# Half of a tile transpose moved from TensorE to VectorE in two places of a two-block fp32 layer

## The reference, cut to what matters

```python
# block 1
mixed = (jax.nn.sigmoid(gate_a) * (o_nsa @ w_branch_a)
         + jax.nn.sigmoid(gate_b) * (z @ w_branch_b))
x = x + mixed @ w_out
# block 2
h = h + (g_conv * y_conv + g_attn * y_attn) @ w_mix_out
```

## Time and profile before

| what | value |
|---|---|
| median of 3 runs | 908.96 us (908.59 to 909.35) |
| the profiled execution | 908.91 us |
| its span, first to last instruction | 907.1 us |
| PE busy | 899.0 us, 99% |
| PE weight loads busy | 773.6 us, 85% |
| DVE busy | 682.9 us, 75% |
| ACT busy | 550.0 us, 61% |
| POOL busy | 33.3 us, 4% |
| granted TensorE clock, mean | 0.999 |

### The profile page before, as it was taken

How to read it: one execution, slowest core, us unless ns; L and a number is a source line. 1 busy time by engine, 2 the same in 40 slices (tenths; PEclk the granted TensorE clock), 3 DMA queues, 4 the chain that set the end, 5 groups by cost and what they waited for, 6 DMA issues and landing times.

```text
span 907.1 us, 13640 instructions
## 1 busy us (share of the span) xinstructions
PE 899.0 (99%) x5005; PEld 773.6 (85%) x5005; DVE 682.9 (75%) x1289; ACT 550.0 (61%) x954; POOL 33.3 (4%) x41
## 2 busy tenths in 40 slices
PE   9999999999999999999999999999999999999997
PEld 7888877788888888888889998888889988888886
DVE  6878975368776666667899999999976776666666
ACT  7756877745654445446666557786845755744454
POOL 0400000000000000000001010010000000000000
PEclk9999999999999999999999999999999999999999
DMA  9955445565555555556798888577564377555551
GB/s 334 317 158 169 147 143 166 184 229 186 165 185 197 198 187 203 194 196 202 225 247 257 195 244 251 136 216 221 188 222 164 99 209 247 189 186 186 186 186 46
DMA packets 95442, 178.22 MB, mean 196 GB/s; under 512 B 7889, under 2 KB 17937, under 8 KB 95121
## 3 DMA queue, kind: packets, MB, share of 16 engines
q1 hardware_dynamic: 92128, 166.35, 56.1%
q0 software_dynamic: 2880, 10.49, 6.1%
q10 hardware_dynamic: 368, 0.52, 0.2%
HBM read 164.69 MB, written 1.05 MB: 183 GB/s over the span
## 4 chain that ended last, share of the span: by engine, by line
PE 97%; DVE 1%; DMA 0%; ACT 0%; issue 0%; SPq 0%; DVEq 0%; ACTq 0%
PE pb L496 95%; PE pb L500 1%; PE pb L710 1%; DVE wlo L1763 1%; DMA raw<-in_w_first 0%; DVE KP L1967 0%; ACT whi L1151 0%; DVE KD L1944 0%; ACT QKV L1151 0%; SPq L426 0%; ACT P L1151 0%; DVE X L2513 0%; DVE ST L1954 0%; DVE CC L2067 0%; DVE MSQ L2551 0%
## 5 line engine op out<-in xcount | busy, mean ns | idle before, releaser
L1763 DVE TENSOR_TENSOR wlo<-raw,whi 128x1024 fp32r<-128x1024 f32 (+1 forms) x278 | 329.2, 1212 | 105.3 <-ACT whi L1151 104.9
L1151 ACT ACTIVATE whi<-raw 128x1024 fp32r<-128x1024 f32 (+2 forms) x304 | 309.1, 1039 | 133.0 <-PE pb L496 120.4
L496 PE MATMUL pb<-XT,whi 128*128 128x512 f32 (+2 forms) x1264 | 285.2, 354 | 1.0 <-DVE CC L2067 1.0
L496 PE MATMUL pb<-whi,ZO 128*128 128x512 f32 (+1 forms) x776 | 239.6, 388 | 0.0
L496 PEld LDWEIGHTS pb<-XT,whi 128*128 128x128 f32 (+1 forms) x1264 | 204.3, 189 | 24.0 <-ACT whi L1151 1.2
L496 PEld LDWEIGHTS pb<-whi,ZO 128*128 128x128 f32 x776 | 145.3, 188 | 29.3
L496 PE MATMUL pb<-XT,wlo 128*128 128x256 f32 (+1 forms) x1032 | 167.5, 282 | 0.0
L496 PE MATMUL pb<-whi,XT 128*128 128x512 f32 (+1 forms) x544 | 165.8, 390 | 0.2 <-ACT whi L1151 0.2
L496 PEld LDWEIGHTS pb<-XT,wlo 128*128 128x128 f32 (+1 forms) x1032 | 153.0, 190 | 13.1
L496 PE MATMUL pb<-wlo,ZO 128*128 128x512 f32 (+1 forms) x388 | 148.9, 388 | 0.0
L496 PEld LDWEIGHTS pb<-whi,XT 128*128 128x128 f32 x544 | 101.1, 188 | 21.3 <-issue 0.9
(11 more groups left out here) (255 smaller groups left out, 648.1 us busy)
## 6 DMA issues: line engine op xcount, KB each, us to landing
raw<-in_w_in SPq DMA_DIRECT2D x105, 512.0 KB, 4.8
raw<-in_w_ff SPq DMA_DIRECT2D x64, 512.0 KB, 5.8
raw<-in_w_up SPq DMA_DIRECT2D x32, 512.0 KB, 4.6
raw<-in_w_down SPq DMA_DIRECT2D x32, 512.0 KB, 4.8
wlo<-raw POOLq DMA_DIRECT2D x20, 512.0 KB, 6.6
raw<-in_w_branch_b SPq DMA_DIRECT2D x8, 512.0 KB, 5.4
raw<-in_w_out SPq DMA_DIRECT2D x8, 512.0 KB, 4.1
raw<-in_wx_kv SPq DMA_DIRECT2D x8, 512.0 KB, 6.0
```

Of the source, the lines that this page charges most:

```text
L496: return e.matmul(o, l, r, start=start, stop=stop, skip_group_check=True)
L1151: return e.activation(o, i, ACT.Copy, scale=scale)
L1763: e.tensor_tensor(wlo[u % NW][:, 0:c], raw_tile(u)[:, 0:c], whi[u % NW][:, 0:c].bitcast(F32), ALU.subtract).then_inc(lo, 1)
```

## The change

The first half of the mixed rows (j = 0, 1; columns 0 to 511) of both blocks no longer goes through TensorE. VectorE transposes it in 32x32 blocks from `GB` (`GC2`) into a new SBUF tile `HB`, whose space is free at both times. One instruction takes 32 partitions: it reads partition group a (32a to 32a + 31) of all four k-tiles and both token tiles, 256 elements of each partition, and writes partition group b, so 16 instructions (a, b = 0 to 3) do a half. They stand in three parts of 5, 5 and 6 at the first three units of `b1_wb1` (`b2_wc1`), each part ahead of that unit's `make_lo`. `make_t_hi` and `make_t_lo` of j = 0 and 1 read `HB` instead of the banks and both move to the step of the fourth unit, on ScalarE and on VectorE. The second half stays as it was. `TURNED` renumbers the semaphore counts.

```diff
@@ TensorE, turn_block1 (turn_block2 alike)
                 yield
-                for j in range(2):
-                    e.wait_ge(mixed, 2)
-                    turn_tiles(T_M1, j, GB)
                 for _ in range(3):
                     yield
...
@@ ScalarE, make_t_hi
-                e.wait_ge(*((turned, 4 * TURN[s] + j + 1) if s != T_FFN else tile_at[f"xo{j // 2}", 2 * (j % 2) + 1]))
+                by_blocks = s in BLOCKS and j < 2
+                e.wait_ge(*((t_blocks, BLOCKS.index(s) + 1) if by_blocks else (turned, TURNED[s, j]) if s != T_FFN else
+                            tile_at[f"xo{j // 2}", 2 * (j % 2) + 1]))
...
-                    copy(d[:, :, 0, :], PB[4 + j][:, :].rearrange("p (k n) -> p k n", k=2)).then_inc(t_hi, 1)
+                    copy(d[:, :, 0, :], HB[:, 2 * j:2 * j + 2, :] if by_blocks else
+                         PB[4 + j][:, :].rearrange("p (k n) -> p k n", k=2)).then_inc(t_hi, 1)
...
@@ VectorE
+            def half_blocks(src, part):
+                d = HB.rearrange("p k (t n) -> p k t n", t=2)
+                v = src.rearrange("p (t k n) -> p k t n", t=2, k=8)
+                for m in range((0, 5, 10)[part], (5, 10, 16)[part]):
+                    a, b = m // 4 * 32, m % 4 * 32
+                    i = e.transpose(d[b:b + 32, :, :, a:a + 32], v[a:a + 32, 0:4, :, b:b + 32])
+                if part == 2:
+                    i.then_inc(t_blocks, 1)
...
@@ VectorE, turn_block1 (turn_block2 alike, with mixed 6 and GC2)
-                yield
+                e.wait_ge(mixed, 2)
+                half_blocks(GB, 0)
+                yield
+                half_blocks(GB, 1)
+                yield
+                half_blocks(GB, 2)
                 yield
                 for j in range(2):
                     make_t_lo(T_M1, j, XT)
-                    yield
+                yield
                 yield
```

More of the change, by code:

```diff
@@ L42 @@
 END_PARTS = (((1, 1, 0, 512), (1, 2, 512, 1024)), ((0, 1, 0, 320), (1, 3, 640, 1024), (0, 2, 320, 640)))
-TURN = {s: i for i, s in enumerate((T_M1, T_2, T_MIX, T_M2, T_XA, T_FFN))}
+BLOCKS = (T_M1, T_M2, )
+TURNED = {sj: i + 1 for i, sj in enumerate((s, j) for s in (T_M1, T_2, T_MIX, T_M2, T_XA) for j in range(4)
+                                           if s not in BLOCKS or j >= 2)}
 GAIN = {T_X: "norm1", T_MEM: "normmem", T_2: "norm2", T_MIX: "normmix", T_XA: "normx", T_FFN: "normffn"}
@@ L111, in build @@
         XS = work(W0 + 4096, "XS", 2048)
+        HB = work(W0 + 2608, "HB", 1024)[:, :].rearrange("p (k n) -> p k n", k=4)
         XG = work(W0 + 16232, "XG", 2056)
@@ L380, in build @@
         z_hi, z_lo = sem("z_hi_made"), sem("z_lo_made")
-        gate, mixed = sem("gates_made"), sem("mixed")
+        gate, mixed, t_blocks = sem("gates_made"), sem("mixed"), sem("half_turned_by_blocks")
         right, h_sq, h_hi, h_lo = sem("right_half_copied"), sem("h_squared"), sem("h_hi_made"), sem("h_lo_made")
@@ L764, in turn_block2 @@
                 yield
-                for j in range(2):
-                    e.wait_ge(mixed, 6)
-                    turn_tiles(T_M2, j, GC2, (ln_var, 1))
                 for _ in range(3):
@@ L771, in turn_block2 @@
                     e.wait_ge(mixed, 8)
-                    turn_tiles(T_M2, j, GC2)
+                    turn_tiles(T_M2, j, GC2, (ln_var, 1))
                 for _ in range(5):
@@ L1832, in make_t_lo @@
                     d = T[:, 2 * j * 512:(2 * j + 2) * 512].rearrange("p (k h n) -> p k h n", k=2, h=2)
-                    e.tensor_tensor(d[:, :, 1, :], PB[4 + j][:, :].rearrange("p (k n) -> p k n", k=2),
+                    e.tensor_tensor(d[:, :, 1, :], HB[:, 2 * j:2 * j + 2, :] if s in BLOCKS and j < 2 else
+                                    PB[4 + j][:, :].rearrange("p (k n) -> p k n", k=2),
                                     d[:, :, 0, :].bitcast(F32), ALU.subtract).then_inc(t_lo, 1)
+            def half_blocks(src, part):
[6 more added lines that the diff above has]
+                    i.then_inc(t_blocks, 1)
             def turn_block1():
@@ L1867, in turn_block2 @@
             def turn_block2():
+                e.wait_ge(mixed, 6)
+                half_blocks(GC2, 0)
                 yield
+                half_blocks(GC2, 1)
+                yield
+                half_blocks(GC2, 2)
                 yield
```

## The result

The changed kernel takes 920.5 us (median of 4 runs, 919.43 to 921.08) against 908.89 (908.59 to 909.35): ratio 1.0127, 95% interval 1.0115 to 1.0139. It is 11.6 us slower, where 6.6 was forecast and 919.0 was the upper end of the range. The profiled execution took 919.43 us with a span of 917.6; both are 10.5 more than in the profiled one of before.

A forecast was written before the change was run, and what follows sets the result against it. TensorE was taken to bound the kernel, busy 899.0 of 907.1 us. Late VectorE results, net of the removed transposes, cost 3.5 us in block 1 and 3.1 in block 2: +6.6, so 915.6 us, range 912.0 to 919.0.

The forecast's parts named there:

- What is removed: Eight TensorE transposes in each block, 0.88 and 0.87 us: 1.75 us gained at most, 0.19% of 908.96.
- The price of a transpose: One new 32-partition transpose on VectorE: 0.42 us from start to start without overlap, 6.7 us in each block.
- The bounds of 0.345 to 0.50: Per new VectorE transpose: 0.345 us with overlap as before, 0.50 with the length of the dearest 128x256 row.
- The place: At `b1_wo0` and block 2's counterpart TensorE stalls 4.0 and 3.7 us, then again for `plus`: +3.5 and +3.1 us.
- The covers: Late weight low parts, raw-buffer loads and ScalarE's high parts all have enough slack before TensorE needs them: cost 0.
- The clock: TensorE's granted clock might halve in the stalls, giving 918 to 919 us; left out of the sum, within a 0.09 chance.
- rival 3: Transposes dearer at 0.50 us, 918.2 us, or TensorE's clock halving in a stall, 918 to 919 us; chance 0.09.
- The sum: Block 1's +3.5 and block 2's +3.1 make +6.6 us: 915.6 us, 0.73% slower.
- Rival 1: Neighbouring new transposes on VectorE overlap, 0.345 us each: +2.1 and +1.7 us, so 912.8 us; chance 0.12.
- rival 2: VectorE transposes two elements at a time from SBUF, 0.367 us each: 913.8 us, with overlap 910.4; chance 0.07.
- Rival 4: Not slower: VectorE's idle time takes the transposes in and 1.75 us is kept, 907.2 us; chance 0.04.
- the 4.4 us: How much less block 1's 16 transposes must take on VectorE to be on time at `b1_wo0`'s first load.

The follow-up runs named there:

- the full-width transposes: Changed kernel with each block's 16 transposes replaced by 4 over all 128 partitions, output differing from the reference: 907.16 us, ratio 0.998.
- kept groups: Changed kernel with each of the 16 transposes writing the partition group it reads, output differing from the reference: 915.61 us, ratio 1.0072.
- changed inputs: Changed kernel with the two transpose loops exchanged, so the input's partition group changes each time and the output's stays for four: 920.84 us, ratio 1.0134.
- the stall filled: Changed kernel with four float32 identity matmuls into an unused bank where TensorE would stand idle in each block: 916.58 us, ratio 1.0084.
- the low part moved: Changed kernel with all 16 transposes and the turned columns' low halves ahead of one more weight low part, both blocks: 915.98 us, ratio 1.0084.

## Why the prediction was wrong

The direction, the queue as the cause and both places were right; the size was not. The step that failed is the clock: its fall behind a stall was left out of the sum and given a share of 0.09, and it fell behind both stalls, which cost 2.5 us at the two places and 3.1 us by the medians.

- **What is removed: right.** 1.75 us computed, 1.6 measured with the full-width transposes.
- **The price of a transpose: a little low.** 0.42 taken, 0.45 measured, 16 x 0.03 = 0.5 us a block. The gap of 0.016 between neighbours was about right (0.436 long, 0.45 apart). The length was not: 0.416 had come from the mean of the 512-element row less 256 elements, and the narrow ones took 0.436. The bounds of 0.345 to 0.50 held it. That a change of group on either side holds the next instruction is shown by the runs with kept groups and with changed inputs; the Trainium skill, page "VectorE: DVE Perf Modes", section "Two Vector instructions with no wait between them", says the same of an input or an output that starts in another quadrant, and this case agrees: 0.45 against the 0.36 that the run with kept groups has on the mean.
- **The place: right.** First turned columns predicted at 212.5, and with the 0.42 of this execution and 0.5 for the transposes that is 213.4; the second of two L1835 starts 0.6 behind the first, so the first, from 212.78, was done at 213.5. `plus` was done at 216.6, predicted 215.65 + 0.42 + 0.5. The two stalls were 4.20 and 3.99 us, against 4.0 and 3.7.
- **The covers: right.** Low parts and loads came late, and TensorE shows no new wait but the two; the moved steps cost nothing by themselves.
- **The clock: the step that failed.** The text had 4.3 us of idling at full clock at the very end of the kernel, called the stalls of 4.0 and 3.7 "just shorter than that", and gave the fall of the clock a share of 0.09 together with dearer transposes. That used one observation as a threshold. In the changed kernel it fell in both blocks, after 4.2 and 4.0 us, and with kept groups after 3.0 and 2.8 us. It is not always so: two runs of that kernel kept a mean of 0.999. And rival 3 reckoned the clock's price as 2.7 us in one unit, on top of the rest. The first unit took 4.41 us instead of 2.72, 1.7 more, and part of that was no loss: behind it stood the wait for `plus`, 0.3 us with the stall filled, which the slow unit hid.
- **The sum.** At the two places 6.6 was forecast. 1.0 more for the length of the transposes would make 7.6, and with the clock kept up they took 7.35. The clock adds 2.5: 9.8. By the medians of one chip it is 7.8 and 3.1, 10.9 together. The 11.6 of the comparison at the head of this document's result holds two runs of four with the clock low for longer.

Rival 1 (overlap) and rival 2 (two elements at a time) were excluded by the 0.45. Rival 3 was nearest, for its second reason; it had the clock fall in one stall and 918 to 919. Rival 4 was right in its kind: with 1.6 us of transposes a block, VectorE's idle time takes them in. One reading in it is off: the 4.4 us is what `plus` asks for in block 1, while `b1_wo0`'s first load asks for the 4.0 of the stall.

No version here beats the kernel before. The only quicker one doesn't move blocks between partition groups, so it doesn't transpose the tile.

## What to carry to other kernels

Work moved to an engine with idle time has to fit ahead of the first result that the bounding engine needs: count the queue up to that instruction, not the busy share. Count instructions, not the partitions that they cover: with 256 elements per partition a transpose over 32 partitions took about as long as one over 128 (0.40 to 0.44 us), so 16 narrow ones took 7.1 us and four wide ones over the same data 1.6, and only 1.2 of the difference was the change of partition group. And price a new stall of TensorE with its clock: of the eleven stalls of 2.7 to 4.2 us in the profiled runs with no filling, ten came with a stretch at half rate, and behind a stall of 4 us that cost 1.2 to 1.5 us more, once 2.3.

## What the runs showed of the hardware

- The granted clock can fall after TensorE has resumed. Of ten falls in the profiled runs nine came 0.1 to 1.5 us after, and the clock was then low for 3.4 us, paid by the matmuls behind. The tenth came 1.6 us before TensorE resumed, and the clock was low for 6.8 us.
- It fell after stalls of 2.8 and 3.0 us in one run of a kernel, and seems not to have fallen (mean 0.999) in two others of the same kernel; with the low part moved it fell after 2.9 us and not after 2.7. Why it stays up in one run and not in the next is open.
- Transposes over 32 partitions of 256 elements start 0.36 us apart on the mean where three neighbours in four keep their groups, and 0.45 where input or output changes group every time. Their recorded length tells less: 0.398 (median) and 0.436, but 128-partition ones that change nothing are recorded at 0.43 to 0.44 too, behind an instruction of another kind.
